# Gated delta net: one matrix for the inverses of both directions, with two products and a turn a level

## The chip, the cores and the metric

The kernel runs on one NeuronCore of one Trainium2 chip. The metric is the device time of one execution in microseconds (us). TensorE (PE in the rows) multiplies matrices and has a queue of its own for loading weights (PEld). VectorE (DVE), ScalarE (ACT) and GpSimd (POOL) do the elementwise work, and SyncE (SP) issues most DMAs. The engines run side by side and wait for one another only through semaphores.

## The reference, cut to what matters

The reference is a trunk of two layers on 512 tokens of width 1024. Layer 0 mixes tokens by windowed attention, layer 1 by a bidirectional gated delta net, and each layer ends with a mixture of 32 experts. The change lies in layer 1's token mixer. Its core is this, once forwards and once on the flipped sequence:

```python
diff = gc[..., :, None] - gc[..., None, :]
decay = jnp.where(tril, jnp.exp(jnp.where(tril, diff, 0.0)), 0.0)
kb = k * beta[..., None]
L = jnp.where(strict, jnp.einsum('bhnid,bhnjd->bhnij', kb, k) * decay, 0.0)
a_mat = L + jnp.eye(C, dtype=L.dtype)
rhs = jnp.concatenate([v * beta[..., None], kb * jnp.exp(gc)[..., None]], axis=-1)
sol = lax.linalg.triangular_solve(a_mat, rhs, left_side=True, lower=True, unit_diagonal=True)
...
def step(state, xs):
    v_new = u_i - jnp.einsum('bhck,bhkv->bhcv', w_i, state)
    o_i = jnp.einsum('bhck,bhkv->bhcv', q_i, state) + jnp.einsum('bhcs,bhsv->bhcv', a_i, v_new)
    state = state * d_i[..., None, None] + jnp.einsum('bhck,bhcv->bhkv', k_i, v_new)
```

There are 8 heads of 128 columns and two directions; the result of both scans is summed, normalised, gated by silu(z) and projected back.

## The kernel before, in words

Everything is one program in float32, with each engine's order of work written out by hand; semaphores `g[...]` join them. The delta net (functions `gdn_pe`, `gdn_act`, `gdn_pool`, `gdn_dve`) works in two halves (`hf`) of four heads. Each half has two parts.

First come 12 units (`UNITS`): q, k and v of four heads, each a projection of 24 matmuls of 512 columns, a convolution on DVE (L1478, L1481), a silu on ACT (L1343), turns on PE (L1204, L1217) and norms. The weights come in panels of 2 MB into a ring (`load_panel`, L1614); ACT and POOL or DVE split each panel into a high and a low part (L161, L167).

Then come four steps `T` of the scan (`scan_pe`, `scan_act`, `scan_pool`, `scan_dve`), with chunks of 128 tokens. A step handles the two directions `d` side by side, chunk T forwards and chunk 3-T backwards, four heads each, so that an operation on one direction has a tile of 128x512 (`[P, HH, P]`) and a bank of PSUM as its output. A step makes for each direction: the products of k with k and q with k and the decay gaps (L1233 to L1236), an exponential (L1382), masks (L1539 to L1551), two turns (L1264), and then the inverse of the unit triangular matrix by doubling blocks of 1, 2, 4 to 64 tokens, in six levels (`LEVELS` is 7). A level has three products of 128x128 for each head: L·X (L1276), a mask on DVE (L1581), then T·W (L1287) and W·T (L1289), since both the inverse (`X`) and its transpose (`T`) are kept; the last level has only the first and the third. ACT copies both results back (L1393, L1394). Last come the solve (L1297), the output (L1305) and the state's update (L1310, L1602). The next step's first products wait for the state and the output of this one.

In the second half's first step ACT and POOL also split panel `GB+7`. After the second half PE projects z in two halves of four units (L1194), while DVE, ACT and POOL normalise the output (L1496 to L1504, POOL's power L1414) and DVE gates it (L1508); then the result is turned (L257) and projected back. The layer's experts follow, whose stage the change leaves alone.

## Time and profile before

| | us |
|---|---|
| median of 3 runs (1743.88 to 1746.6) | 1746.36 |
| the profiled execution, its own time | 1746.1 |
| span of its records | 1744.5 |
| PE busy in the span | 1440.5 |
| PE busy from 787.4 to 986.5, the four steps of the first half from their first level on | 185.46 of 199.1 |

The profiled execution took 1746.1 us, 0.3 under the median, so terms read from it can be set against the median as they are. The span leaves out 1.6 us around the first and the last record. A matmul's duration in the rows is longer than the distance to the next one, since they are pipelined: the distance of starts is what one costs. The four starts that structure the text: the first half's units end at about 765.8, its four steps at 986.5 when the second half's first unit starts; the second half's units end at about 1072.1 and its steps at 1294.6.

### The profile page before, as it was taken

Reading aid. Unit: us, or ns where it says so; the run is one execution under the profiler, and the core shown is the slowest. Engines: PE = TensorE matmul, PEld = TensorE weight load, DVE = VectorE, ACT = ScalarE, POOL = GpSimd, SP = SyncE. Lnnn points to the kernel's source line nnn. Section 1 sums busy time; section 2 is a strip of 40 time slices with the busy share of each in tenths; the row PEclk is TensorE's granted clock in tenths of the full one; section 3 lists DMA queues with packets and bytes.
Section 4 is the critical chain, followed back from the end, with each engine's and each line's share of the span. In section 5 each row is a group of like instructions: output and inputs, shape, how many; then the busy total and the mean of one; then the engine's idle time right before and its main releaser. Section 6 shows DMA issues by size and latency. Waiting matters only on the chain. (4 is left out here: it accounts for less than half of the span.)

```text
span 1744.5 us, 22611 instructions
## 1 busy us (share of the span) xinstructions
PE 1440.5 (83%) x9233; PEld 1125.2 (65%) x9233; DVE 641.8 (37%) x1390; ACT 420.2 (24%) x819; POOL 394.7 (23%) x369
## 2 busy tenths in 40 slices
PE   6899995598788558889999987999999957888883
PEld 4767785355445257668888866888887754544551
DVE  3557514111111152764454376455435221111113
ACT  4246410101001123333323343333233101100110
POOL 1220003322221220521111053231114042222210
PEclk9999995699999856989999999999999958999997
DMA  5210005499999900210000012000003246999996
GB/s 183 97 49 1 19 25 217 156 386 397 397 391 399 351 31 0 92 53 1 1 1 1 1 69 77 1 1 1 1 1 109 79 162 243 390 399 394 387 411 234
DMA packets 66232, 270.87 MB, mean 155 GB/s; under 512 B 17132, under 2 KB 17388, under 8 KB 41552
## 3 DMA queue, kind: packets, MB, share of 16 engines
q1 hardware_dynamic: 49744, 237.86, 35.2%
q0 software_dynamic: 12064, 21.32, 3.6%
q10 hardware_dynamic: 4320, 10.23, 1.7%
q8 instruction: 75, 1.23, 0.3%
q14 instruction: 29, 0.24, 0.0%
HBM read 262.78 MB, written 23.35 MB: 164 GB/s over the span
## 5 line engine op out<-in xcount | busy, mean ns | idle before, releaser
L850 PE MATMUL bank<-ring,arena 128*64 128x256 f32 x2048 | 261.4, 408 | 73.1 <-issue 71.8
L850 PEld LDWEIGHTS bank<-ring,arena 128*64 128x64 f32 x2048 | 168.5, 141 | 147.0 <-issue 84.9
L735 POOL DMA_INDIRECT y_rows<-arena,idx_i x64 | 64.1, 1002 | 405.6 <-DVE arena L1008 397.6
L1289 PE MATMUL bank<-arena 128*128 128x128 f32 x768 | 140.6, 276 | 0.0
L1012 DVE TENSOR_TENSOR arena<-arena,bank 128x128 f32<-128x128 f32 x64 | 18.4, 288 | 326.3 <-ACT arena L927 326.3
L1287 PE MATMUL bank<-arena 128*128 128x128 f32 x640 | 124.5, 276 | 3.8 <-DVE arena L1581 3.8
L1581 DVE TENSOR_TENSOR arena<-bank,arena 128x512 f32<-128x512 f32 x96 | 65.5, 689 | 167.6 <-PE bank L1276 167.6
L859 PE MATMUL bank<-ring,arena 128*64 128x512 f32 x512 | 123.9, 604 | 1.5 <-DVE arena L1017 1.5
L927 ACT ACTIVATE arena<-bank 128x128 f32<-128x128 f32 x64 | 17.7, 277 | 423.5 <-PE bank L850 386.2
L1276 PE MATMUL bank<-arena 128*128 128x128 f32 x768 | 106.3, 281 | 12.7 <-ACT arena L1394 10.8
L145 PE MATMUL bank<-ring_r,ht_r 128*128 128x512 f32 x288 | 113.3, 393 | 0.0
L1289 PEld LDWEIGHTS bank<-arena 128*128 128x128 f32 x768 | 112.7, 192 | 0.7
L1276 PEld LDWEIGHTS bank<-arena 128*128 128x128 f32 x768 | 93.2, 191 | 21.8 <-ACT arena L1394 18.4
L1287 PEld LDWEIGHTS bank<-arena 128*128 128x128 f32 x640 | 97.1, 192 | 5.3 <-DVE arena L1581 5.3
L1008 DVE COPY arena<-bank 128x512 f32<-128x512 f32 x64 | 44.3, 692 | 144.7 <-PE bank L859 144.7
L167 POOL TENSOR_TENSOR ring_r<-ring,ring_r 128x1024 fp32r<-128x1024 f32 x36 | 90.5, 2538 | 25.4 <-ACT ring_r L161 25.4
L257 PE MATMUL bank<-ident,hn 128*128 128x128 f32 x192 | 40.6, 383 | 66.3 <-DVE hn L241 59.9
L143 PE MATMUL bank<-ring_r,arena_r 128*128 128x512 f32 x224 | 89.8, 401 | 4.3 <-DVE ring_r L167 4.3
L144 PE MATMUL bank<-ring_r,arena_r 128*128 128x512 f32 x224 | 88.4, 395 | 0.0
L842 PEld LDWEIGHTS bank<-ident,arena 64*128 64x128 f32 x512 | 61.3, 201 | 34.7 <-issue 25.1
L1393 ACT COPY arena<-bank 128x512 f32<-128x512 f32 x80 | 46.8, 585 | 151.6 <-PE bank L1289 151.6
L257 PEld LDWEIGHTS bank<-ident,hn 128*128 128x128 f32 x192 | 33.5, 212 | 73.1 <-DVE hn L241 56.1
(260 smaller groups left out, 2619.0 us busy)
## 6 DMA issues: line engine op xcount, KB each, us to landing
ring<-in_moe_w_gate SPq DMA_DIRECT2D x64, 1024.0 KB
ring<-in_moe_w_up SPq DMA_DIRECT2D x64, 1024.0 KB
ring<-in_moe_w_down SPq DMA_DIRECT2D x64, 1024.0 KB
ring<-in_gdn_w_in SPq DMA_DIRECT2D x8, 2048.0 KB
arena<-y_rows ACTq DMA_DIRECT2D x16, 512.0 KB, 7.4
ring<-in_attn_w_in SPq DMA_DIRECT2D x3, 2048.0 KB
ring<-in_attn_w_out SPq DMA_DIRECT2D x2, 2048.0 KB
h_rows<-hn POOLq DMA_DIRECT2D x8, 512.0 KB, 11.8
```

The costliest lines, as they stand in the source:

```text
L143: pe.matmul(dst, a[0], b[0], start=start, stop=False)
L144: pe.matmul(dst, a[0], b[1], start=False, stop=False)
L145: return pe.matmul(dst, a[1], b[0], start=False, stop=stop)
L167: eng.tensor_tensor(panel(n, False, True)[:, c, :], panel(n)[:, c, :], panel(n, True, True)[:, c, :].bitcast(F32), ALU.subtract).then_inc( ...
L257: last = pe.transpose(b[:, j * P:(j + 1) * P], hn[:, t, half * 4 + j::KC], ident[:, :])
L735: pool.indirect_dma_start(out=y_rows[l], out_offset=bass.IndirectOffsetOnAxis(ap=idx_i[:, 1, e:e + 1], axis=0), in_=y_out[:, e % RING, :], ...
L850: last = pe.matmul(bank[1][m * SLOTS:(m + 1) * SLOTS, 0:2 * P].rearrange("p (w n) -> p w n", w=2), xgt[:, i, c * SLOTS:(c + 1) * SLOTS], w ...
L859: last = pe.matmul(bank[3][half * SLOTS:(half + 1) * SLOTS, :], hidden_t[:, i, m * SLOTS:(m + 1) * SLOTS], d[:, m, half * HALF:(half + 1) ...
L1276: last = pe.matmul(bank[3 * d][:, h * P:(h + 1) * P], buf["L"][d][:, h, :], buf["X"][d][:, h, :], start=True, stop=True)
L1287: pe.matmul(bank[3 * d + 1][:, h * P:(h + 1) * P], buf["T"][d][:, h, :], buf["W"][d][:, h, :], start=True, stop=True)
L1289: last = pe.matmul(bank[3 * d + 2][:, h * P:(h + 1) * P], buf["W"][d][:, h, :], buf["T"][d][:, h, :], start=True, stop=True)
L1581: dve.tensor_tensor(buf["W"][d], heads_of(bank[3 * d]), by_head(level[l][:, d, :]), ALU.mult).then_inc(g["w"], 1)
```

## The change

One matrix per chunk and head now serves both directions: its lower triangle belongs to the forward scan and its upper to the backward one. The inverses are built apart from the scan, for two chunks at a time (two `slot`s; chunks 0 and 3, then 1 and 2), and kept with the masked q·k products in the ring's free panel. A level has one product with a masked matrix `lm` (POOL), `I - product` on DVE, a second product, and a turn of a tile `s` that ACT copies back; which half of the result goes on is chosen by two columns of constants, `stay` and `move`, one or the other for each row. `r` and `s` are updated by a copy with a factor (ACT) or a multiply by a column (POOL) and a fused multiply-add (DVE). The scan then has steps `n` without levels; step 0 has no products with the state, the last none that update it. The decays come from one product with a constant triangle for each direction and 512 columns (`rows_pe`), an exponential with beta's logarithm as its bias, and a triangular select on POOL. `w_in`'s fifth panel is loaded when the first half's scan is over, and panel `GB+7` after the second's; its split moves into the z projection. The constants and small vectors are prepared by a few other small operations, and the norm's four semaphores become two.

```diff
+        lm, w_buf, r_even, r_odd, s_buf, st_buf = [[gl.take(HH, P) for _ in range(2)] for _ in range(6)]
+        r_buf = (r_even, r_odd)
+        rhs_in, solved, q_part, e_own = w_buf, r_even, st_buf, st_buf
...
+        def kept(hf, at):
+            at = (GB + hf) % 2 * PAIR + at * HH * P
+            return flat_ring[0][:, at:at + HH * P].rearrange("p (h n) -> p h n", h=HH)
...
+                pe.wait_ge(g["kt"], 8 * (hf + 1))
+                rows_pe(pe, 4 * hf, (6, 7))
+                pe.wait_ge(g["u"], 12 * hf + 12)
+                prods_pe(pe, 4 * hf, (0, 2))
                 to_tokens_pe(pe, UNITS[12 * hf + 11])
-                for T in range(4 * hf, 4 * hf + 4):
-                    scan_pe(pe, T, hf)
-            pe.wait_ge(g["s"], 16)
+                pe.wait_ge(g["tok"], 12 * hf + 12)
+                rows_pe(pe, 4 * hf + 1, (1, 4))
+                prods_pe(pe, 4 * hf + 1, (3, 5))
+                pe.wait_ge(g["exps"], 8 * hf + 2)
+                rows_pe(pe, 4 * hf + 2, (6, 7))
+                inverse_pe(pe, 2 * hf)
+                inverse_pe(pe, 2 * hf + 1)
+                for n in range(TT):
+                    scan_pe(pe, hf, n)
...
+        def rows_pe(pe, n, banks):
+            pe.wait_ge(g["gi"], n + 1)
             for d in range(DIRS):
...
+        def prods_pe(pe, n, banks):
+            c = cols(chunk_of(n))
+            four(pe, banks[0], lambda h: k_tr[:, h, c], lambda h: k_tr[:, h, c])
+            four(pe, banks[1], lambda h: k_tr[:, h, c], lambda h: q_tr[:, h, c]).then_inc(g["prods"], 1)
...
+        def inverse_pe(pe, p):
+            first = p % 2 == 0
+            if first:
+                pe.wait_ge(g["exps"], 4 * p + 4)
+                for slot in range(2):
+                    first_m(pe, 2 * p + slot, 3 * slot + 1)
+            for l in range(1, LEVELS):
+                for slot in range(2):
+                    pe.wait_ge(g["r"], at_level(p, l, slot))
+                    pe.wait_ge(g["lm"], at_level(p, l, slot))
+                    four(pe, 3 * slot, lambda h: lm[slot][:, h, :], lambda h: r_buf[l % 2][slot][:, h, :]
+                         ).then_inc(g["y"], 1)
+                if first and l == 1:
+                    pe.wait_ge(g["exps"], 4 * p + 6)
+                    rows_pe(pe, 2 * p + 3, (6, 7))
+                if first and l == 2:
+                    pe.wait_ge(g["exps"], 4 * p + 8)
+                    prods_pe(pe, 2 * p + 2, (6, 7))
+                if first and l == 4:
+                    pe.wait_ge(g["a"], 2 * p + 3)
+                    prods_pe(pe, 2 * p + 3, (6, 7))
+                for slot in range(2):
+                    if l >= 2:
+                        pe.wait_ge(g["sn"], at_level(p, l - 1, slot))
+                        if l == 2 and not first:
+                            pe.wait_ge(g["se"], at_level(p - 1, LEVELS - 1, slot))
+                        turn_four(pe, 3 * slot + 2, s_buf[slot]).then_inc(g["t"], 1)
+                    elif not first:
+                        last_m(pe, p - 1, slot)
+                for slot in range(2):
+                    pe.wait_ge(g["wc"], at_level(p, l, slot))
+                    if l >= 2:
+                        pe.wait_ge(g["se"], at_level(p, l - 1, slot))
+                    four(pe, 3 * slot + 1, lambda h: st_buf[slot][:, h, :], lambda h: w_buf[slot][:, h, :]
+                         ).then_inc(g["un"], 1)
+            for slot in range(2):
+                if first:
...
+        def scan_pe(pe, hf, n):
+            if n == 0:
+                pe.wait_ge(g["se"], 24 * hf + 24)
+            else:
+                for d in range(DIRS):
+                    c = cols(chunk(n, d))
+                    pe.wait_ge(g["s"], 6 * hf + 2 * (n - 1) + d + 1)
+                    pe.wait_ge(g["o2"], 8 * hf + 2 * (n - 1) + d + 1)
+                    four(pe, 4 * d, lambda h: k_tr[:, h, c], lambda h: state[:, d, h * P:(h + 1) * P]
+                         ).then_inc(g["ks"], 1)
+                for d in range(DIRS):
+                    c = cols(chunk(n, d))
+                    if n >= 2:
+                        pe.wait_ge(g["qc"], 6 * hf + 2 * (n - 2) + d + 1)
+                    four(pe, 4 * d + 1, lambda h: q_tr[:, h, c], lambda h: state[:, d, h * P:(h + 1) * P]
+                         ).then_inc(g["qs"], 1)
             for d in range(DIRS):
...
+                if n:
+                    pe.wait_ge(g["rr"], 6 * hf + 2 * (n - 1) + d + 1)
+                four(pe, 4 * d + 2, lambda h: inverse_of(hf, d)[:, h, :],
+                     lambda h: rhs_in[d][:, h, :] if n else v_tok2[:, h, chunk(n, d), :]).then_inc(g["ys"], 1)
+            if n < TT - 1:
+                for d in range(DIRS):
+                    pe.wait_ge(g["kd"], 6 * hf + 2 * n + d + 1)
+                    pe.wait_ge(g["yc"], 8 * hf + 2 * n + d + 1)
+                    four(pe, 4 * d + 3, lambda h: k_decayed(hf, d)[:, h, :], lambda h: solved[d][:, h, :]
+                         ).then_inc(g["su"], 1)
             for d in range(DIRS):
...
+                pe.wait_ge(g["yc"], 8 * hf + 2 * n + d + 1)
+                four(pe, 4 * d, lambda h: a_kept(hf, chunk(n, d), d)[:, h, :], lambda h: solved[d][:, h, :]
+                     ).then_inc(g["av"], 1)
...
-                    elif t in (1, 2):
-                        split_high(act, GB + 8, (2 * t - 2, 2 * t - 1))
+                    if t in (1, 2):
+                        split_high(act, GB + 7 + half, (2 * t - 2, 2 * t - 1))
...
+        def inverse_act(act, p):
+            first = p % 2 == 0
+            for l in range(1, LEVELS):
+                if l < LEVELS - 1:
+                    for slot in range(2):
+                        act.wait_ge(g["r"], at_level(p, l, slot))
+                        if l >= 2:
+                            act.wait_ge(g["rb"], at_level(p, l - 1, slot))
+                        act.activation(flat(r_buf[(l + 1) % 2][slot]), flat(r_buf[l % 2][slot]), ACT.Copy,
+                                       scale=stay[:, l:l + 1]).then_inc(g["ra"], 1)
+                if first and l == 1:
+                    exps_act(act, 2 * p + 3, (6, 7))
+                for slot in range(2):
+                    if l >= 2:
+                        act.wait_ge(g["t"], at_level(p, l - 1, slot))
+                        act.copy(flat(st_buf[slot]), bank[3 * slot + 2][:, :]).then_inc(g["se"], 1)
+                    elif not first:
+                        last_m_act(act, p - 1, slot)
+            if not first:
+                for slot in range(2):
+                    last_m_act(act, p, slot)
...
+        def keep_pool(pool, p, l, slot):
+            pool.wait_ge(g["r"], at_level(p, l, slot))
+            if l >= 2:
+                pool.wait_ge(g["t"], at_level(p, l - 1, slot))
+            elif p % 2:
+                pool.wait_ge(g["t"], at_level(p - 1, LEVELS - 1, slot))
+            if l < LEVELS - 1:
+                pool.tensor_scalar(s_buf[slot], r_buf[l % 2][slot], move[:, l:l + 1], None, ALU.mult
+                                   ).then_inc(g["rb"], 1)
+            else:
+                pool.affine_select(out=s_buf[slot], in_=r_buf[l % 2][slot], compare_op=ALU.not_equal, fill=0.0,
...
+                        if not first:
+                            pool.wait_ge(g["y"], at_level(p - 1, LEVELS - 1, slot))
+                    else:
+                        pool.wait_ge(g["y"], at_level(p, l - 1, slot))
+                    pool.tensor_tensor(lm[slot], lt_of(n), by_head(level[l]), ALU.mult).then_inc(g["lm"], 1)
+                if l >= 2:
+                    for slot in range(2):
+                        keep_pool(pool, p, l - 1, slot)
+                if first and l == 1:
+                    spread_pool(pool, 2 * p + 3)
+                    select_pool(pool, 2 * p + 2)
+                if first and l == 3:
+                    select_pool(pool, 2 * p + 3)
+                if first and l in (4, 6):
+                    diag_pool(pool, 2 * p + l // 2)
+            for slot in range(2):
...
+        def scan_pool(pool, hf, n):
+            if n == 0:
+                pool.wait_ge(g["se"], 24 * hf + 24)
             for d in range(DIRS):
...
+                if n:
+                    pool.wait_ge(g["ys"], 8 * hf + 2 * (n - 1) + d + 1)
+                triangle(pool, inverse_of(hf, d), m_kept(hf, chunk(n, d)), d).then_inc(g["xs"], 1)
...
+                first_r(dve, n + 1, 4)
+            third, fourth = 2 * p + 2, 2 * p + 3
+            for l in range(1, LEVELS):
+                for slot in range(2):
...
+                    o.step(sum_e(dve, fourth))
+                if first and l == 5:
+                    make_a(dve, fourth, 7, 0)
+                if l < LEVELS - 1:
+                    for slot in range(2):
+                        dve.wait_ge(g["un"], at_level(p, l, slot))
+                        dve.wait_ge(g["ra"], under_six(p, l, slot))
+                        r = flat(r_buf[(l + 1) % 2][slot])
+                        dve.scalar_tensor_tensor(out=r, in0=bank[3 * slot + 1][:, :], scalar=move[:, l:l + 1], in1=r,
+                                                 op0=ALU.mult, op1=ALU.add).then_inc(g["r"], 1)
+                    for slot in range(2):
+                        dve.wait_ge(g["rb"], at_level(p, l, slot))
+                        dve.scalar_tensor_tensor(out=flat(s_buf[slot]), in0=bank[3 * slot + 1][:, :],
+                                                 scalar=stay[:, l:l + 1], in1=flat(s_buf[slot]),
+                                                 op0=ALU.mult, op1=ALU.add).then_inc(g["sn"], 1)
+                else:
+                    for slot in range(2):
+                        dve.wait_ge(g["un"], at_level(p, l, slot))
+                        dve.wait_ge(g["rb"], at_level(p, l, slot))
+                        dve.tensor_tensor(flat(s_buf[slot]), bank[3 * slot + 1][:, :], flat(s_buf[slot]), ALU.add
...
             sp.wait_ge(s["up"], 30)
...
-                load_panel(sp, GB + 6 + i, w_in[:, :, at:at + PANEL], (g["proj"], 20 + 4 * i))
+                load_panel(sp, GB + 6 + i, w_in[:, :, at:at + PANEL], ((g["proj"], 20), (g["av"], 16))[i])
...
```

## Rows read from the trace of the kernel before

**Rows 1.** The page: busy time of the engines, the slices of PE and its clock
```profile
PE 1440.5 (83%) x9233; PEld 1125.2 (65%) x9233; DVE 641.8 (37%) x1390; ACT 420.2 (24%) x819; POOL 394.7 (23%) x369
PE   6899995598788558889999987999999957888883
PEclk9999995699999856989999999999999958999997
```

**Rows 2.** Windows: stretch, its length, busy time (records) of PE, PEld, DVE, ACT, POOL, clock, DMA
```profile
765.90:787.40 21.50, 14.45 (x105) 13.43 (x105) 13.28 (x31) 4.86 (x7) 2.42 (x3) 0.84 0.28 98
787.40:986.50 199.10, 185.46 (x1570) 178.15 (x1569) 87.85 (x222) 64.11 (x117) 32.32 (x30) 1.00 0.00 1
852.40:858.30 5.90, 5.63 (x51) 5.44 (x50) 2.42 (x6) 2.15 (x4) 0.00 (x0) 1.00 0.01 4
```

**Rows 3.** Timeline of PE, one level to the next, and turns: start, us, line, records
```profile
852.46 1.06 PE L1276 MATMUL bank<-arena 128*128 128x128 f32 x8
853.79 1.16 PE L1276 MATMUL bank<-arena 128*128 128x128 f32 x8 [0.27 <-ACT arena L1394]
...
858.36 1.06 PE L1276 MATMUL bank<-arena 128*128 128x128 f32 x8
...
839.08 1.06 PE L1264 MATMUL bank<-ident,arena 128*128 128x128 f32 x8 [0.70 <-DVE arena L1551]
839.98 1.06 PE L1276 MATMUL bank<-arena 128*128 128x128 f32 x8
```

**Rows 4.** Timeline of PE in the expert stage: float32 products of 512 columns
```profile
401.04 1.94 PE L859 MATMUL bank<-ring,arena 128*64 128x512 f32 x8
402.90 0.33 PE L892 MATMUL bank<-ident,arena 128*128 128x128 f32 x1
```

**Rows 5.** Timeline of DVE and ACT in the same level
```profile
853.56 0.69 DVE L1581 TENSOR_TENSOR arena<-bank,arena 128x512 f32<-128x512 f32 x1 [2.74 <-PE bank L1276]
...
852.66 0.58 ACT L1393 COPY arena<-bank 128x512 f32<-128x512 f32 x1 [0.71 <-PE bank L1289]
853.14 0.59 ACT L1394 COPY arena<-bank 128x512 f32<-128x512 f32 x1
```

**Rows 6.** Timelines of DVE, with POOL's splits beside it and without; and both engines
```profile
1004.75 1.47 DVE L1478 TENSOR_SCALAR arena<-arena 128x512 f32<-128x512 f32 x1 [0.45 <-ACT arena L1335]
1006.25 4.34 DVE L1481 SCALAR_TENSOR_TENSOR arena<-arena 128x512 f32<-128x512 f32 x3
1022.01 0.48 DVE L1478 TENSOR_SCALAR arena<-arena 128x512 f32<-128x512 f32 x1
1022.53 2.33 DVE L1481 SCALAR_TENSOR_TENSOR arena<-arena 128x512 f32<-128x512 f32 x3
...
789.64 0.68 DVE L1581 TENSOR_TENSOR arena<-bank,arena 128x512 f32<-128x512 f32 x1
789.77 1.04 POOL L1429 TENSOR_TENSOR arena<-arena 128x512 f32<-128x512 f32 x1
```

**Rows 7.** Groups of POOL by line: count, busy us, mean ns
```profile
L1425 POOL TENSOR_TENSOR arena<-arena 128x512 f32<-128x512 f32 x16 | 24.6, 1537 | 2.3 <-ACT arena L1385 1.4
L1433 POOL TENSOR_TENSOR arena<-arena 128x512 f32<-128x512 f32 x16 | 16.3, 1039 | 254.7 <-ACT arena L1397 254.7
L1421 POOL TENSOR_SCALAR_AFFINE_SELECT arena<-arena 128x512 f32<-128x512 f32 x16 | 12.6, 788 | 102.2 <-DVE arena L1544 102.2
L586 POOL TENSOR_SCALAR arena<-arena 128x384 f32<-128x384 f32 x16 | 11.4, 715 | 54.5 <-DVE arena L531 53.9
L1414 POOL TENSOR_TENSOR arena<-arena,mhalf 128x8 f32<-128x8 f32 x4 | 10.2, 2546 | 20.8 <-DVE arena L1498 20.8
```

**Rows 8.** Groups of DVE and ACT with 128 columns: count, busy us, mean ns
```profile
L1602 DVE SCALAR_TENSOR_TENSOR arena<-arena,bank 128x128 f32<-128x128 f32 x64 | 18.0, 344 | 2.9 <-PE bank L1310 2.4
L927 ACT ACTIVATE arena<-bank 128x128 f32<-128x128 f32 x64 | 17.7, 277 | 423.5 <-PE bank L850 386.2 <-issue 37.3
```

**Rows 9.** Timeline between the last unit's projection and the first step
```profile
770.71 0.63 ACT L1343 ACTIVATE arena<-arena 128x512 f32<-128x512 f32 x1 [2.92 <-DVE arena L1481]
771.36 1.28 ACT L1382 ACT_TABLE_LOAD   x1
...
771.40 1.11 PE L1204 MATMUL bank<-ident,arena 128*128 128x128 f32 x4 [3.36 <-ACT arena L1343]
```

**Rows 10.** Timeline of DVE at the end of the z projection
```profile
1339.07 1.72 DVE L1508 TENSOR_TENSOR hn<-hn,arena 128x1024 f32<-128x1024 f32 x1 [3.96 <-ACT arena L1352]
```

**Rows 11.** The load of a w_in panel, 762 to 776: GB/s in 40 slices
```profile
GB/s 0 0 0 0 0 0 0 0 0 0 0 0 0 0 0 135 123 252 351 392 398 410 415 398 392 427 398 415 415 386 374 269 41 0 0 47 0 0 0 0
```

533 lines of the change are left out of this document (288 added, 245 removed), and 5 rows, old and new, of the table g.

## The prediction

> **What bounds the kernel now.** I read the page first. PE is busy 83% of the span, the other engines 22 to 37% [rows 1], and its slices are full from about 785 us to 985 and again from 1090 to 1290, where the clock stands at its higher level of 2.4 GHz. These are the eight steps of the delta net's scan. The windows say it exactly: from the first step's first level to the end of the first half PE is busy 185 of 199 us, DVE 88, ACT 64, POOL 32 [rows 2]. So this stage is PE's, and what counts is how many products it issues.
>
> The price of a product comes from the timeline of PE. Eight records of L1264 are eight turns and take 0.90 us to the next group [rows 3], so a record costs 0.11 us. A product of 128x128 is two records (768 of L1276 for 8 steps x 6 levels x 8 tiles): 0.22, four of them 0.89. One level lasts from 852.46 to 858.36, 5.90 us, with 24 products (5.34) in it; the rest is the wait for ACT's copies. A step is thus 5 x 24 + 16 products for its levels and 64 besides, 200 in all (44.5 us), plus 16 turns (1.8): 46.3. Four steps make 185, which is the window's busy time.
>
> With setup, a half costs 986.5 - 765.8 = 220.7 and 1294.6 - 1072.1 = 222.5, together 443.2 us. This is what the change can touch.
>
> **PE's work after.** For each half: 2 pairs x 6 levels x 16 products (42.7), 112 turns (12.4: 16 first, 80 within the levels, 16 last), 4 x 8 products for k·k and k·q (7.1), and the scan's 136 products (24 + 24 with the state, 32 solves, 24 updates, 32 outputs: 30.3). The decays are eight products of 512 columns; in the expert stage four such products fill 1.86 us from 401.04 to 402.90 [rows 4], so 0.93 for each chunk, 3.7. Sum 96.2 us against 185 plus its share of setup. If PE stayed the only bound, two halves would save 180 or more. But now each level is a chain through four engines, so I lay it out.
>
> **A level.** A bank is ready for DVE 1.10 after its first product starts (852.46 to 853.56) [rows 3, 5]. A DVE operation on 128x512 takes 0.69 and lets PE go after 0.73; back to back they come every 0.60, and for the multiply-add with a column I take 0.78 and 0.64, as the 128-column form is 0.05 slower than its plain neighbours at 0.29 (an estimate from L1602's 0.344) [rows 8]. ACT copies take 0.58, every 0.48, seen by PE after 0.65 [rows 5]. Let the second product of slot 0 start at A, slot 1's at A+0.89. Then `r` is updated from A+1.10 and A+1.99, the next first products start at A+1.88 and A+2.77, `s` is updated from A+2.63 and A+3.27, and the turns go at A+3.66 and A+4.10. ACT's copy of the first turn starts at A+4.31, PE sees it at A+4.96. DVE's `I - product` starts at A+3.91, is seen at A+4.64, so the copy ends last. The period is **5.0 us**, of which PE works 4.45 (16 products, 8 turns). It serves two chunks in both directions, where 5.90 served two of the four.
>
> POOL does two masked products and two multiplies by a column in a level. The nearest rows of the first are L1425 at 1.54 and L1433 at 1.04; for the second L586, 0.715 on 384 columns, so 0.95 on 512, and the select L1421, 0.79 [rows 7]. That makes 3.7 to 5.0 us, at or below the period; I take 1.2 and 0.8, because L1425 always runs beside DVE work on two SBUF tiles. I charge POOL nothing, its cover being the level itself; if a column multiply costs what L1425 costs, POOL needs 6.2 and sets the period.
>
> *Two pages against the trace.* DVE's multiply-adds on SBUF take 4.34 for three while POOL splits a panel and 2.33 when it does not; L1581, which reads one bank, takes 0.68 beside POOL's L1429 [rows 6]. The Trainium skill, "SBUF — State Buffer", "SBUF: two separate sides", says that a DVE instruction with two SBUF inputs and a GpSimd one exclude each other for their whole length. By that rule the level's six DVE operations, each with a bank as an input, run free, and the trace agrees. The Trainium skill, "GPSIMD Engine Reference", "4.1 Engine selection", speaks against this change: elementwise work on two inputs belongs on VectorE, being about twice as slow on GpSimd. With its 2.6 cycles for an element at 1.2 GHz a masked product would be 1.1 us plus dispatch (an estimate from that page), near the lower row, and the sum would stay.
>
> **A half, step by step.** Setup: as before, silu of the last unit ends at 771.34 and the exponential's table is loaded by 772.64 [rows 9]. Eight exponentials of 128 columns (0.28 each, about 0.18 apart [rows 8]) 1.5; POOL's select 0.8, two decay operands for chunk 2 2.3, the second select 1.5, DVE's sum and product 1.3, the unit diagonal and the seed 1.4, then 1.2 for two masks that stand ahead in DVE's queue and 1.3 for the first `st` and `r`: the first level starts at about 783.9, **18** after the units' end (21.7 before). The first pair: 6 x 5.0, plus what is queued between its products on PE: decays 0.9, two groups of k·k and k·q 1.8 each, and DVE's and POOL's extra operations at levels 1, 3, 5 and 6, 3.0: **37.5**. Changeover with first masks **1.6**, second pair **30**, last turns and copies **1.5**. Scan: step 0 has a select, a solve, ACT's copy, update and output, 6.5. A middle step has ten groups of four products, 8.9 on PE; the next step's first bank is freed by DVE's addition, at 9.3; two of them 18.6. The last has no update, 8.7. Sum **33.8**. Together 122.4; I add 1.6 for waits that I have not listed: **124**.
>
> **Around it.** The loads: the fifth w_in panel was loaded in the scan's shadow and is now issued when the first half's last output product is done. A panel takes about 6 us [rows 11]. Its first split stands in ACT's queue about 10 us after the next unit starts, ahead of the next unit's copy, so it costs nothing; if the load were slower by 4 us, each us more would be paid. Tail: panel `GB+7`'s low part (four operations of 2.5 us on POOL, as L167 has it) now stands ahead of the four powers of 2.55 [rows 7], and ends about 24 us after the scan. From there power, reduction and scaling, 5.2 for each of four tiles, end at 44, and four gates of 1.22 at 48.8. Before, the last gate ended at 1340.8, 46.2 after [rows 10]. So **+2.6**. The masks are made while DVE waits in the routing stage: 0. The small vectors trade a reciprocal for two or three short operations: 0.
>
> 1746.1 - 443.2 + 2 x 124 + 2.6 = **1553** (1553.5). The profiled run is 0.3 under the median, which I neglect. Changes under 0.2%, 3.5 us, can't be told from none here.
>
> **Rivals.**
> - *POOL sets the period.* The column multiply is not in the trace. At 1.54 each the level is 6.2, 24 levels x 1.2 = 29: 1582. For it: every engine now feeds the next. Against it: the select and L586 are cheap [rows 7].
> - *The chain is as slack as the old level*, 5.9 for 5.0, through waits that my table misses: 24 x 0.9 = 22, 1575.
> - *DVE and POOL exclude each other even with a bank as an input*: 3.7 + 3.6 = 7.3 a level, +55, 1608. Rows 6 speak against it.
> - *The clock.* PE idles more often. In the setup before, busy 14.5 of 21.5 us, the granted clock was 0.84 [rows 2]. If the whole stage ran at 1.2 GHz, PE's 96 become 192 and a half about 212: 1729.
> - *Loads come late*: 5 us at the second half's start and as much at the tail: 1563.
> - *Slower.* POOL has one slow operation, the power: 2.55 us for 8 columns [rows 7]. If its multiply by a column ran by such a loop, it would decide from 5.4 us on: then a level is 2 x 1.15 + 2 x 5.4 = 13.1, 24 x 8.1 = 194, and the gain is gone; beyond that it is slower, say 1760.
>
> **How the numbers follow.** Chances: forecast 0.60, POOL 0.14, slack chain 0.11, loads 0.05, exclusion 0.03, clock 0.04, slow multiply 0.03. Low end: levels at PE's own 4.45 (-13) and none of the unlisted waits (-3): 1537, taken as 1534. High end: POOL's 1582 with 8 for loads, 1590. That leaves out the last three cases and the edges of the others, less than 2 in 10. Faster: all but the last and a little of the clock's, 0.96; same 0.01; slower 0.03.
>
> **What would show it.** In the profile after: in the second pair of each half a level every 5.0 us with PE busy 4.45; first products after the units' end by 18 us; a middle scan step of 9.3; POOL's masked product near 1.2 and column multiply near 0.8; the stretch between units and next stage 124 instead of 221; the expert stages unchanged. I am wrong if the masked or column operations on POOL are above 1.25 on average, if `y` waits for POOL rather than for DVE, or if the clock in the stage is well under 1.

## The result and the profile after

The changed kernel takes 1589.24 us (median of 4 runs, 1584.3 to 1591.8) where the kernel before, timed beside it, takes 1746.32. The ratio is 0.910, 95% interval 0.9076 to 0.9124. It is faster by 157 us, where 193 were forecast. It stands within the range, 0.8 us under its upper end of 1590, and 36 us above the forecast. The profiled execution was the fastest of the four, 1584.3 us, span 1582.7; all that is read from it below stands against 1553, a miss of 31.

The page of the changed kernel, first its engines, its slices and its chain (compare [rows 1]):

```profile
PE 1276.8 (81%) x7601; PEld 950.4 (60%) x7601; DVE 631.7 (40%) x1196; ACT 382.8 (24%) x796; POOL 523.1 (33%) x476
...
POOL 1321001332212114024788336786350342221210
PEclk8999999589999995589899999899989669999997
...
PE bank L865 8%; PE bank L874 4%; PE bank L1286 2%; PE bank L857 2%; PE bank L143 1%; PE bank L144 1%; PE bank L145 1%; POOL arena L1566 1%; DMA arena<-y_rows 1%; DVE hn L1700 1%; POOL arena L1529 1%; PE bank L907 0%; POOL arena L719 0%; DVE hn L1696 0%; POOL slot_table L728 0%
```

PE is nearly as full as before over the whole span (81% for 83), but POOL is now at seven and eight tenths in two stretches where it was nearly idle, and POOL's L1566, the new column multiply, stands in the chain that ended last. Now the stage cut into its parts (windows: busy time of PE, weight loads, DVE, ACT, POOL, granted clock; compare [rows 2]):

```profile
765.90:788.20 22.30, 13.41 (x60) 8.83 (x61) 17.70 (x22) 10.27 (x29) 14.66 (x15) 0.86 0.01 1
788.20:832.50 44.30, 38.20 (x279) 34.89 (x277) 33.39 (x49) 13.85 (x28) 37.44 (x31) 0.91 0.00 1
832.50:867.20 34.70, 31.59 (x248) 28.08 (x248) 24.41 (x36) 14.85 (x24) 29.12 (x23) 1.00 0.00 1
867.20:902.00 34.80, 32.17 (x273) 31.03 (x273) 17.40 (x54) 10.89 (x32) 15.84 (x18) 1.00 0.00 1
844.84:850.39 5.55, 5.07 (x42) 4.52 (x41) 4.10 (x6) 2.50 (x4) 5.55 (x6) 1.00 0.00 0
850.39:855.94 5.55, 5.08 (x42) 4.53 (x41) 4.10 (x6) 2.50 (x4) 5.55 (x6) 1.00 0.00 0
883.46:893.28 9.82, 9.40 (x81) 9.08 (x81) 5.53 (x19) 3.24 (x10) 3.67 (x4) 1.00 0.01 2
```

The four first rows are the terms of my sum for one half. Forecast and measured, in us:

| term | forecast | measured |
|---|---|---|
| setup, to the first product of a level | 18 | 22.3 |
| first pair and changeover | 37.5 + 1.6 | 44.3 |
| second pair, last turns and copies | 30 + 1.5 | 34.7 |
| scan | 33.8 | 34.8 |
| waits not listed | 1.6 | - |
| first half | 124 | 136.1 |

The second half with its projections went from 308.1 us (986.5 to 1294.6) to 222.9 (902.0 to 1124.9), 85.2 saved for 98.5 forecast; the first half saved 84.6 for 96.7. What follows the delta net's last step took 449.9 before (1294.6 to 1744.5) and takes 457.8, which is +7.9 for the +2.6 forecast. So 25 us are missing in the two halves and 5 behind them.

The windows show one thing more. The granted clock stands at 0.50, that is 1.2 GHz, from 785.5 to 792.3, after a stretch in which PE was mostly idle, and the first products of a level fall into it; shorter falls follow. Windows of the changed kernel, in the same form: the first products, the sixth level of the first pair with the next one, in the first and the second half, and the stretch from the second pair's last masked product to the half's end, in the first and the second half:

```profile
788.24:791.66 3.42, 3.42 (x18) 3.42 (x17) 1.78 (x3) 0.72 (x1) 3.42 (x4) 0.50 0.00 0
817.86:833.74 15.88, 12.12 (x89) 11.24 (x87) 14.15 (x22) 3.23 (x7) 10.31 (x10) 0.89 0.00 1
1039.56:1055.00 15.44, 10.73 (x89) 9.69 (x87) 14.34 (x22) 3.23 (x7) 10.76 (x9) 1.00 0.01 2
855.93:901.97 46.04, 41.51 (x344) 38.84 (x343) 24.83 (x65) 15.02 (x39) 22.76 (x25) 1.00 0.00 1
1077.22:1124.87 47.65, 43.14 (x344) 40.46 (x343) 24.79 (x61) 16.30 (x40) 22.83 (x25) 0.96 0.00 1
```

Sixteen records take 3.42 us in the first row, where 0.11 each makes 1.78; the second half has the same. The two levels cost 0.44 more where the clock fell, and the scan 1.6. Together this is some 5 us of the 25 (an estimate from these rows: 2 x 1.64, 0.44 and 1.61).

In the table of seven windows further up, the fifth and sixth rows each show one level of the second pair: 5.55 us, and POOL busy in all of it. The timelines of that level say what it does and who waits for it:

```profile
845.73 0.66 PE L1291 MATMUL bank<-ident,arena 128*128 128x128 f32 x4 [0.48 <-DVE arena L1786]
846.32 4.05 PE L1286 MATMUL bank<-arena 128*128 128x128 f32 x32
...
844.92 0.75 DVE L1786 SCALAR_TENSOR_TENSOR arena<-bank,stay,arena 128x512 f32<-128x512 f32 x1 [0.66 <-POOL arena L1566]
845.59 1.28 DVE L1769 TENSOR_TENSOR arena<-ident,bank 128x512 f32<-128x512 f32 x2
847.52 1.64 DVE L1782 SCALAR_TENSOR_TENSOR arena<-bank,move,arena 128x512 f32<-128x512 f32 x2 [0.65 <-PE bank L1286]
...
844.84 2.52 POOL L1591 TENSOR_TENSOR arena<-ring,arena 128x512 f32<-128x512 f32 x2
847.32 3.12 POOL L1566 TENSOR_SCALAR arena<-arena,move 128x512 f32<-128x512 f32 x2
```

POOL goes from two masked products (2.52 us) straight to two column multiplies (3.12) and from there to the next level, with no gap. DVE's update of `s` waits 0.66 us for the multiply, and PE's turn waits 0.48 for that update. The multiply costs twice what I gave it (`count | busy us, mean ns`):

```profile
L1566 POOL TENSOR_SCALAR arena<-arena,move 128x512 f32<-128x512 f32 x40 | 63.2, 1595 | 2.6 <-PE bank L1291 2.6
L1591 POOL TENSOR_TENSOR arena<-ring,arena 128x512 f32<-128x512 f32 x48 | 62.0, 1317 | 8.1 <-PE bank L1286 8.1
```

### The profile page after: what moved, and what is told of

The parts are those of the page before. It is cut to its first block and busy times, and to the rows that moved or that the text cites. A ratio compares the mean times of both kernels' runs of the same rounds, so it can differ in the third digit from the quotient of the medians.

```text
span 1582.7 us, 19352 instructions
## 1 busy us (share of the span) xinstructions
PE 1276.8 (81%) x7601; PEld 950.4 (60%) x7601; DVE 631.7 (40%) x1196; ACT 382.8 (24%) x796; POOL 523.1 (33%) x476
## 5 line engine op out<-in xcount | busy, mean ns | idle before, releaser
L1286 PE MATMUL bank<-arena 128*128 128x128 f32 x1088 | 140.4, 286 | 14.3 <-DVE arena L1769 6.5
L1286 PEld LDWEIGHTS bank<-arena 128*128 128x128 f32 x1088 | 131.7, 198 | 26.6 <-DVE arena L1769 10.0
L167 POOL TENSOR_TENSOR ring_r<-ring,ring_r 128x1024 fp32r<-128x1024 f32 x36 | 93.9, 2632 | 34.8 <-ACT ring_r L161 34.8
L1023 DVE COPY arena<-bank 128x512 f32<-128x512 f32 x64 | 44.3, 692 | 144.6 <-PE bank L874 144.6
L257 PEld LDWEIGHTS bank<-ident,hn 128*128 128x128 f32 x192 | 33.8, 213 | 84.1 <-DVE hn L241 58.5
L857 PEld LDWEIGHTS bank<-ident,arena 64*128 64x128 f32 x512 | 61.3, 201 | 34.7 <-issue 25.1
L1673 DVE SCALAR_TENSOR_TENSOR arena<-arena 128x512 f32<-128x512 f32 x72 | 80.9, 1123 | 2.6
L144 PE MATMUL bank<-ht_r,ring_r 128*128 128x512 f32 x192 | 78.0, 406 | 0.0
L857 PE MATMUL bank<-ident,arena 64*128 64x64 f32 x512 | 70.1, 278 | 9.3 <-DMA arena<-h_rows,idx_i 9.3
L743 POOL DMA_INDIRECT arena<-h_rows,idx_i x64 | 60.7, 948 | 25.7 <-issue 18.9
L229 POOL TENSOR_TENSOR norm_s<-norm_s,mhalf 128x1 f32<-128x1 f32 x16 | 8.9, 556 | 171.3 <-DVE norm_s L238 171.3
L1591 POOL TENSOR_TENSOR arena<-ring,arena 128x512 f32<-128x512 f32 x48 | 62.0, 1317 | 8.1 <-PE bank L1286 8.1
```

The costliest lines, as they stand in the source:

```text
L144: pe.matmul(dst, a[0], b[1], start=False, stop=False)
L167: eng.tensor_tensor(panel(n, False, True)[:, c, :], panel(n)[:, c, :], panel(n, True, True)[:, c, :].bitcast(F32), ALU.subtract).then_inc( ...
L257: last = pe.transpose(b[:, j * P:(j + 1) * P], hn[:, t, half * 4 + j::KC], ident[:, :])
L857: last = pe.transpose(bank[0][:, c * SLOTS:(c + 1) * SLOTS], xg[0:SLOTS, i, c::KC], ident[0:SLOTS, 0:SLOTS])
L1286: last = pe.matmul(bank[b][:, h * P:(h + 1) * P], lhs(h), rhs(h), start=True, stop=True)
L1591: pool.tensor_tensor(lm[slot], lt_of(n), by_head(level[l]), ALU.mult).then_inc(g["lm"], 1)
```

## The experiments

The rival "POOL sets the period" looked true at this point, and its price, 29 us, looked like the whole miss. The first experiment tests it; the others take the remaining places where the windows show lost time. Each is timed beside the kernel before, and since the runs come from different chips, I compare ratios: two of them can be told apart from about 0.0021 on, 3.7 us.

**The changed kernel again**, as the yardstick.

> The changed kernel once more, as the yardstick for the runs beside it: 1584 to 1592 us, ratio to the kernel before 0.910.

1587.44 us, ratio 0.9081 (0.9067 to 0.9096). From the first masked product of the first pair to that of the second pair: 44.4 us, and 44.6 in the second half; the second pair's levels 5.56.

**The column multiply on ACT.**

```diff
-                pool.tensor_scalar(s_buf[slot], r_buf[l % 2][slot], move[:, l:l + 1], None, ALU.mult
+            act.activation(flat(s_buf[slot]), flat(r_buf[l % 2][slot]), ACT.Copy, scale=move[:, l:l + 1]
```

> The column multiply that keeps part of the matrix at a level (POOL, two a level, 1.6 us each) is done by ACT with a column as its scale; POOL keeps the masked product alone (two of 1.26). If POOL's 5.6 us a level set the 5.55 us period, the levels of the second pairs come every 5.0 to 5.1 us (PE's own records fill 5.07 of the 5.55), those of the first pairs lose 1 us and more each, and the kernel gains 12 to 20 us: 1567 to 1575. If the chain of matmul, DVE and turn sets it and POOL is only busy beside it, the period stays within 0.1 us of 5.55 and the time within 2 us of the changed kernel's. If ACT becomes the bound (4.1 us of work a level by the rows after), the period stays above 5.3.

1584.20 us, 0.9065 (0.9049 to 0.9081): 2.8 us by the ratios, which alone could be nothing. The trace is clear, though. Timelines of POOL and of PE's and ACT's part in one level:

```profile
846.93 2.52 POOL L1602 TENSOR_TENSOR arena<-ring,arena 128x512 f32<-128x512 f32 x2 [2.71 <-PE bank L1286]
852.16 2.51 POOL L1602 TENSOR_TENSOR arena<-ring,arena 128x512 f32<-128x512 f32 x2 [2.71 <-PE bank L1286]
...
848.95 4.03 PE L1286 MATMUL bank<-arena 128*128 128x128 f32 x32 [0.33 <-ACT arena L1488]
...
849.17 1.34 ACT L1568 ACTIVATE arena<-arena,move 128x512 f32<-128x512 f32 x2
```

The level now comes every 5.23 us and POOL waits 2.71 in it. So POOL did set the period, but the next bound stands only 0.32 us behind it. In the first pair nearly nothing changed: 44.0 and 43.6 us for 44.4 and 44.6. My expectation of 12 to 20 us was wrong there. The rival's mechanism is real and its price is not: something else holds the first pair. One part of that is the clock. The second level of the first pair, in the two halves of this same run:

```profile
794.26:800.80 6.54, 6.54 (x37) 4.93 (x36) 2.41 (x5) 2.94 (x10) 2.49 (x3) 0.81 0.00 0
1015.86:1020.87 5.01, 5.01 (x34) 3.92 (x34) 2.42 (x5) 2.94 (x10) 2.50 (x3) 1.00 0.00 0
```

PE is busy in all of both, and the one at the lower clock takes 1.5 us more.

**What makes the multiply dear.** First a constant for the column (the kernel then leaves out the choice of rows, and only its times mean anything), then, with the column back, a second step that adds zero, then both.

```diff
-                pool.tensor_scalar(s_buf[slot], r_buf[l % 2][slot], move[:, l:l + 1], None, ALU.mult
+                pool.tensor_scalar(s_buf[slot], r_buf[l % 2][slot], 0.5, None, ALU.mult
```

> POOL's column multiply takes the constant 0.5 instead of the column of the level, so the inverse is wrong and only times are read. If reading the multiplier from a column is what costs, the operation falls from 1.56 us (3.12 for two) to near my 0.8, POOL has 4.1 us a level and the level comes every 5.2 us as it did with the multiply on ACT: 3 us gained. If 128x512 costs 1.56 in any form, nothing changes: 1587.

```diff
-                pool.tensor_scalar(s_buf[slot], r_buf[l % 2][slot], move[:, l:l + 1], None, ALU.mult
+                pool.tensor_scalar(s_buf[slot], r_buf[l % 2][slot], move[:, l:l + 1], 0.0, ALU.mult, ALU.add
```

> The same column multiply on POOL, written as multiply by the column and then add 0.0, the form of the 384-column operation that I priced it by (0.51 us at its fastest; only that form's second step differs). The result is the same. If the form with a second step is the cheap one on POOL, the operation falls from 1.58 us to 0.7 to 0.8, POOL has 4.1 us a level, and the level comes every 5.2 us: 3 us gained, as with the multiply on ACT. If a second step adds work, it is 1.6 us or more and the level 5.6 or longer: 1587 or more.

> Multiply by the constant 0.5 and add 0.0 (the inverse is wrong, only times are read): exactly the form of the 384-column operation. If the row's price carries over by columns, 0.7 to 0.8 us. If it stays at 1.5, that row was cheap for another reason than its form.

The line's own view (minimum, median and maximum in ns, then who waited for it), first of the constant without a second step, then of the column with one, then of the constant with one:

```profile
L1566 POOL TENSOR_SCALAR arena<-arena x40: 1481/1491/1928, 796.3 to 1084.0; 128x512 f32<-128x512 f32 x40
```

```profile
L1566 POOL TENSOR_SCALAR arena<-arena,move x40: 688/697/1135, 794.3 to 1078.8; 128x512 f32<-128x512 f32 x40
```

```profile
L1566 POOL TENSOR_SCALAR arena<-arena x40: 612/621/1057, 796.4 to 1082.3; 128x512 f32<-128x512 f32 x40
```

Reading the multiplier from a column costs 0.08 us (0.70 to 0.62, or 1.58 to 1.49). The missing second step costs 0.87: `multiply` is slower than `multiply, then add 0.0`. The row by which I priced the operation, L586 in [rows 7], has a second step, and the diff's line has `None` there. The times: 0.9066 (0.905 to 0.9083) for the constant with levels of 5.39 us; 1581.13 us, 0.9043 (0.9017 to 0.9069) for the column with the second step, levels of 5.23 as on ACT, and nobody waits for POOL's multiply any more; the last one had one run, 1585.18, levels 5.23. One argument in one line gives 6.6 us with an interval of about 5. In the traces it does what the multiply on ACT did: from the last projection's end to the next stage the halves take 134.5 and 135.1 us here, 134.4 and 135.0 there. So 6.6 and 2.8 are two readings of one gain.

The Trainium skill, "GPSIMD Engine Reference", "4.1 Engine selection", says that against VectorE GpSimd is about twice as slow with two tensor inputs and roughly at line rate with one. By that rule the multiply would be well below the masked product. These runs agree when the operation has its second step (0.62 to 0.70 for 1.28) and contradict it when it has not (1.49 to 1.58, above the masked product).

**DVE's extra work in the first pair.** PE's timeline of the yardstick in the last levels of the first pair, and DVE's:

```profile
812.24 2.05 PE L1286 MATMUL bank<-arena 128*128 128x128 f32 x16 [1.27 <-DVE ring L1730]
...
822.47 4.06 PE L1286 MATMUL bank<-arena 128*128 128x128 f32 x32 [2.02 <-DVE arena L1769]
...
828.93 0.38 PE L1286 MATMUL bank<-arena 128*128 128x128 f32 x1 [1.53 <-DVE arena L1769]
...
819.54 0.68 DVE L1727 TENSOR_TENSOR ring<-bank,ring 128x512 f32<-128x512 f32 x1
820.14 1.68 DVE L1735 TENSOR_TENSOR ring<-ring,arena 128x512 f32<-128x512 f32 x1
821.74 1.27 DVE L1769 TENSOR_TENSOR arena<-ident,bank 128x512 f32<-128x512 f32 x2
```

The product of the fourth chunk's k·k with its decay (L1727) and the third chunk's seed (L1735) stand in DVE's queue ahead of `I - product` (L1769), for which PE waits 2.02 us. The seed has two SBUF inputs and takes 1.68 for 0.68, as POOL's masked products run from 818.77 to 821.27. Seven of the ten extra operations stand like this between the update of `s` and the next `I - product`. The edit moves them behind L1769, where DVE waits for PE anyway, and the fourth chunk's two decay products into the second pair. It also moves PE's two groups for the fourth chunk behind the second products of the fourth level; the two moves were not tried apart. Cut to a part:

```diff
-                if first and l == 4:
-                    make_lt(dve, fourth, 6)
-                    make_v0(dve, third)
...
+                if first and l == 5:
+                    make_lt(dve, fourth, 6)
+                    make_v0(dve, third)
...
+                if not first and l == 2:
+                    make_a(dve, 2 * p + 1, 7, 0)
```

> The ten DVE operations on the third and fourth chunk that stand within the first pair's levels move to where DVE waits for the second product of a level (two of them into the second pair's levels), and PE's products for the fourth chunk move behind the level's last ones. From the first masked product to the second pair's first masked product the changed kernel takes 44.4 us. If DVE's queue order is what makes these levels long (waits of 1.3, 2.0 and 1.5 us of PE for it), it takes 40 us or less, and the kernel gains 7 to 10 us: near 1579. If POOL or PE's own extra products set them, it stays above 43 and the time within 3 us of 1587.

1578.53 us, 0.9035 (0.9022 to 0.9047): 8.0 us faster than the yardstick, the largest single gain. The pair takes 41.9 and 41.4 us for 44.4 and 44.6, so 2.6 and 3.2 gained, with the clock at 0.92 in all four: less than expected within the pair. The rest is not in these levels. From the second pair's last masked product to the end of the first half, the yardstick and then this run:

```profile
856.47:903.99 47.52, 42.98 (x344) 40.34 (x343) 24.82 (x65) 15.02 (x39) 22.85 (x25) 0.96 0.00 1
854.93:900.96 46.03, 41.50 (x344) 38.83 (x343) 24.83 (x65) 15.02 (x39) 22.79 (x25) 1.00 0.00 1
```

The work is the same and the clock is not, and the second half shows the same 1.5 us. The changed kernel's own trace has this stretch once at 46.0 and once at 47.7, so it is not the edit's doing as far as the traces show. DVE's order, with PE's, is worth some 6 of the 8 us.

**POOL's spreads later, and another order at a half's start.**

```diff
+            if n % 4 < 2:
+                pool.wait_ge(g["conv"], 12 * hf + 11 + n % 4)
             for d in range(DIRS):
                 last = pool.tensor_tensor(e_of(n)[d], by_head(incl_of(1 - d)), col("g", c, hf, d), ALU.mult)
```

> POOL's two spreads of the gate over the triangle wait for the convolutions of the last two units. If they shut DVE out of a convolution (5.66 us for three multiply-adds, 2.33 without), the eleventh unit's convolution ends over 2 us sooner and the first levels start 1 to 1.5 us sooner in each half: 2 to 3 us gained. If the stretch is set by ACT's table load and exponentials in turn, nothing changes within 1 us, and if the second spread comes late for the second chunk's rows, up to 2 us are lost.

```diff
                 make_v0(dve, n)
-                make_a(dve, n + 1, 5, 0)
-                make_a(dve, n + 1, 5, 1).then_inc(g["a"], 1)
-                first_st(dve, n)
-                first_r(dve, n, 1)
                 make_v0(dve, n + 1)
-                first_st(dve, n + 1)
+                first_r(dve, n, 1)
                 first_r(dve, n + 1, 4)
+                first_st(dve, n)
+                first_st(dve, n + 1)
+                make_a(dve, n + 1, 5, 0)
+                make_a(dve, n + 1, 5, 1).then_inc(g["a"], 1)
```

> At the start of a half DVE makes both seeds (v0), then both first r, both first st, and only then the second chunk's two decay products. If the setup's 22.4 us were set by DVE's queue order, PE's second turn starts 2 us sooner and so do the levels: 2 to 2.5 us less from the last projection to the first product of a level in each half, 4 to 5 us in all, 1583. If ACT's exponentials and POOL's diagonal set it, less than 1 us a half.

The spreads: 1587.81 us, 0.9086 (0.9072 to 0.9099), no gain. DVE's timeline in the yardstick and in the experiment, with POOL's in the second:

```profile
762.68 5.66 DVE L1673 SCALAR_TENSOR_TENSOR arena<-arena 128x512 f32<-128x512 f32 x3
769.51 1.01 DVE L1670 TENSOR_SCALAR arena<-arena 128x512 f32<-128x512 f32 x1 [0.57 <-ACT arena L1413]
```

```profile
764.43 4.34 DVE L1675 SCALAR_TENSOR_TENSOR arena<-arena 128x512 f32<-128x512 f32 x3
769.95 1.29 DVE L1672 TENSOR_SCALAR arena<-arena 128x512 f32<-128x512 f32 x1 [0.57 <-ACT arena L1413]
...
768.92 2.04 POOL L1548 TENSOR_TENSOR arena<-arena 128x512 f32<-128x512 f32 x2 [2.27 <-DVE arena L1675]
```

The eleventh unit's multiply-adds became 1.3 us shorter (not 3.3, since a panel's low part still ran beside them), and then the twelfth unit's multiply met the spread (1.29 for 1.01) that POOL now makes from 768.92 on. The first masked product comes 18.7 and 18.5 us after the last projection's end, for 19.2 and 18.1.

The order: 0.9072 (0.9056 to 0.9087), 1.6 us by the ratios, not resolved. The first product of a level starts 2.5 us after the first masked product instead of 4.4, as expected, but the second pair then starts only 1.2 us sooner in each half. POOL's masked products of the second level start 7.0 us after those of the first in both kernels, behind a spread and two selects, so the first level gains nothing. Of the 1.2 us, 0.9 come in the second level, where the granted clock is 1.00 for 0.82. The order and the clock may hang together: in all eight halves with this order (here and in the three kernels that combine edits, below) the fall at the first products lasts 3.4 us, in 15 of the 18 halves without it 6.8. So DVE's queue did delay the first product, but what the sooner start gave by itself and what by a shorter fall of the clock was not separated.

**The tail.** Timelines of DVE and POOL in the changed kernel (compare [rows 10]):

```profile
1170.12 10.97 DVE L1700 TENSOR_TENSOR hn<-hn,arena 128x1024 f32<-128x1024 f32 x4
...
1138.59 4.77 POOL L167 TENSOR_TENSOR ring_r<-ring,ring_r 128x1024 fp32r<-128x1024 f32 x2 [15.68 <-ACT ring_r L161]
...
1148.75 1.66 POOL L1529 TENSOR_TENSOR arena<-arena,mhalf 128x8 f32<-128x8 f32 x1
...
1164.11 2.54 POOL L1529 TENSOR_TENSOR arena<-arena,mhalf 128x8 f32<-128x8 f32 x1 [2.87 <-DVE arena L1690]
1166.62 12.26 POOL L167 TENSOR_TENSOR ring_r<-ring,ring_r 128x1024 fp32r<-128x1024 f32 x4
```

POOL's powers begin 24 us after the z projection's start (1124.9), as forecast. But then the next panel's low part begins at 1166.62 and runs beside the gates: four gates take 10.97 us.

```diff
+            pool.wait_ge(g["ready"], TT)
             split_low(pool, GB + 8)
```

> POOL's low part of the first output panel (four of 2.5 to 3.1 us) waits until DVE has made the four gates. If POOL shuts DVE out of the gates (10.97 us for four, 1.1 us each without it), the gates end some 7 us sooner after the z projection's start (at +49 instead of +56), the last quarters of the panel then come about 1.5 us late for PE, and the kernel gains 4 to 6 us. If the gates are slow for another reason, they still take 11 us, and the kernel loses about 10 us, since the panel's low part comes after them.

1581.99 us, 0.9053 (0.9038 to 0.9067): 4.9 us gained. The same two engines:

```profile
1170.84 4.63 DVE L1701 TENSOR_TENSOR hn<-hn,arena 128x1024 f32<-128x1024 f32 x4
...
1175.55 9.41 POOL L167 TENSOR_TENSOR ring_r<-ring,ring_r 128x1024 fp32r<-128x1024 f32 x4 [6.07 <-DVE hn L1701]
```

Both engines are faster apart than together: 4.63 for 10.97 and 9.41 for 12.26. Each of the first three gates takes 3.25 to 3.38 beside POOL, about its own 1.16 and one subtraction's 2.35. PE's first product of the projection comes 51.6 us after the z projection's start (1127.7 to 1179.3) instead of 60.9 (1124.9 to 1185.7), and some of that is given back since the panel's low part is now late for it. The Trainium skill, "SBUF — State Buffer", "SBUF: two separate sides", says that a DVE instruction with two SBUF inputs and a GpSimd instruction that reads SBUF exclude each other for their whole length. The gates have two SBUF inputs, and this pair of runs agrees with it. So DVE and POOL wait for one another not only through semaphores. PE's waits at the turns before the projection fell too, from 9.9 us to 3.1, and with them the time at 1.2 GHz there, from 17.1 us (1171.2 to 1188.3) to 3.4.

**The four together**, with the multiply on ACT.

> The multiply on ACT, the panel's low part behind the gates, DVE's work in its waits and the start's order, together. If the four act on different stretches their gains add: 3.2 and 5.5 measured, 8 and 4.5 expected, 1566 to 1569. If the multiply on ACT was held back by DVE's extras in the first pair, up to 5 us more: 1561. If ACT becomes the bound, 1572 or more.

1565.56 us, 0.8957 (0.8939 to 0.8975), 21.7 us below the yardstick by the ratios, just under the 1566 to 1569 expected for gains that add. The single gains (2.8, 4.9, 8.0, 1.6) add up to 17, with an uncertainty of about 11, as the yardstick's own error stands in each of them; so the surplus of 4 us is not resolved. The first pair takes 37.9 us, 6.5 less than the yardstick, where the three edits that touch it gave 0.4, 2.5 and 1.2 alone. Some 1.6 of the 2.4 us that the single gains leave open sit in the second level: 6.5 us in the yardstick with the clock at 0.82, 5.6 with the start's order at full clock but with POOL's dear multiply, 5.0 with the multiply on ACT at full clock, 4.0 here. There the multiply and the late start with its slower clock had covered for each other. The other 0.8 sit in the fifth and sixth levels, where the multiply on ACT alone lost 0.7, DVE's order alone gave 2.7 and both together 2.8.

**The same with the multiply on POOL and its second step**, and then with the spreads too as multiplies by a column:

```diff
-                last = pool.tensor_tensor(e_of(n)[d], by_head(incl_of(1 - d)), col("g", c, hf, d), ALU.mult)
+                for h in range(HH):
+                    last = pool.tensor_scalar(e_of(n)[d][:, h, :], incl_of(1 - d), one("g", c, hf, d, h), 0.0,
+                                              ALU.mult, ALU.add)
```

> The four changes of the run before together, but with the multiply left on POOL and given its second step (0.70 us) instead of moved to ACT. If the level is now the chain of PE, ACT's copy and DVE, and POOL only has to be under it, the level comes every 5.23 us as with ACT, and the time is that of the run before within 2 us: 1564 to 1568.

> The same, and the spread of the gate over the triangle is made of four multiplies by a column of 128x128 with a second step instead of one product of two tiles of 128x512 (1.24 us each, 16 in all). If such a multiply is as cheap as the others here (0.7 us for 512 columns, so 0.2 to 0.3 for 128), a spread takes 0.8 to 1.1 us, and if it leaves DVE free, DVE's sum of the decays beside it takes 0.69 instead of 1.52 and the eleventh unit's last three multiply-adds 2.33 instead of 5.66: the first level starts 1 to 2 us sooner in each half, 2 to 4 us gained. If issue costs are high, four take as long as one and nothing is gained.

1565.45 us, 0.8969 (0.8957 to 0.8981), levels 5.23 and first pair 37.9: as with ACT, and as expected. With the spreads 1563.75 us, 0.8955 (0.8942 to 0.8967), 2.4 us less, within the uncertainty. The traces show no gain: the first masked product comes 0.3 to 1.0 us sooner and the first pair takes 38.7 for 37.9. Both are faster than the kernel before and the changed one. In the last of them POOL's groups, and then the timelines of POOL and DVE in the setup:

```profile
L1569 POOL TENSOR_SCALAR arena<-arena,move 128x512 f32<-128x512 f32 x40 | 29.1, 740 | 1.4 <-PE bank L1291 1.4
L1548 POOL TENSOR_SCALAR ring<-arena 128x128 f32<-128x128 f32 x48 | 21.6, 472 | 0.0
```

```profile
776.24 0.90 POOL L1548 TENSOR_SCALAR ring<-arena 128x128 f32<-128x128 f32 x1
...
776.29 0.69 DVE L1726 TENSOR_TENSOR ring<-arena 128x512 f32<-128x512 f32 x1
```

A 128-column multiply takes 0.37 us alone (the mean, 0.47, has some that waited), and four of them 1.7 to 1.9 (2.4 beside the eleventh unit's multiply-adds), more than the 1.24 to 1.46 of the product that they replace. DVE's sum beside them takes 0.69 where it took 1.52 beside the product. But DVE is not free of POOL: the multiply that started at 776.24 took 0.90, so here POOL waited for DVE's sum, and then went on. Shorter instructions changed who waits, and for how long. The expected 0.2 to 0.3 was wrong.

## Why the prediction was right and where it was wrong

**Right.** The stage was PE's, and its products were what it paid for: with the inverses of both directions in one matrix a half goes from 221 us to 136. The scan came at 34.8 for 33.8, a middle step at 9.82 for 9.3, with PE busy 9.40 of it. POOL's masked product takes 1.28 in the median, 1.32 in the mean, for 1.2. The clock stood at 0.86, 0.91 and 1.00 in the stage's parts, so the rival with the whole stage at 1.2 GHz is out; a smaller price of the clock is not (the sixth step below). Late loads are out: the second half's projections took 84.2 us for 85.9 before. DVE's six level operations, each with a bank as an input, were not held up by POOL: 1.28, 1.64 and 1.4 to 1.5 us for pairs beside a POOL that never rests, and 1.27, 1.64 and 1.40 with the multiply on ACT and POOL idle for 2.71 of 5.23.

**Luck.** The range held by 0.8 us, and not for its reasons. Its upper end was POOL's 29 and 8 for late loads; curing POOL gave 6.6 and the loads cost nothing, and terms that the range had no name for filled the place. Two of the prediction's own signs of being wrong came true: both POOL operations are above 1.25 us on average, 1.32 and 1.59.

**The step that failed first** is "for the second L586, 0.715 on 384 columns, so 0.95 on 512 ... I take 1.2 and 0.8" and with it "I charge POOL nothing". The multiply took 1.59. I scaled a row whose form was not the form of the diff. POOL then needs 5.6 us a level and set the period. The rival that says so was right in its mechanism, and its price (1.2 us for each of 24 levels, 29 us) was wrong: with the multiply at 0.70, or on ACT, the second pair's level is 5.23, so POOL cost 0.32 there, and the whole cure gave 6.6 us by one reading and 2.8 by the other.

**The second** is the period of **5.0**. It is 5.23 when POOL is out of the way. My table had every hand-over, and PE's wait for ACT's copy of the turn, 0.33, is the one that it shows too; PE's own groups follow each other with small gaps where the table had none. At 0.23 for each of 24 levels this is 5.5 us.

**The third**, and the largest that one edit gave back, is "DVE's and POOL's extra operations at levels 1, 3, 5 and 6, 3.0", in a first pair of 37.5. It took 44.3 with the changeover, for 39.1 (37.5 and 1.6). I summed durations and did not place them in the queue: seven of the operations stand between the update of one level and the first operation of the next, and PE waits for what is behind them. Their order gave 2.6 and 3.2 us back. With DVE's order, the start's and POOL's multiply mended, the stretch from masked product to masked product is 37.9 for 44.4. A second term of this pair was wrong as well, "decays 0.9": the price came from [rows 4], whose products have 64 columns of weights where these have 128. PE's rows of one chunk's decays at full clock, the next product starting at 777.36:

```profile
775.54 1.12 PE L1300 MATMUL bank<-ring,arena 128*128 128x512 f32 x2 [0.78 <-DVE arena L1707]
776.51 1.02 PE L1300 MATMUL bank<-ring,upper 128*128 128x512 f32 x2
```

That is 1.82 us for 0.93. One chunk of four is queued in the first pair, among products that PE runs without a gap from 787.34 to 799.29, and costs 0.9 more there.

**The fourth** is setup, 18 for 22.3. Eight exponentials took 2.18 us, not 1.5; the decays of three chunks took some 1.8 us of PE each, where 0.9 was my price; DVE's sum took 1.52 for 0.69 beside POOL's spread; the first turn of the second chunk waited for its seed behind two products. Later spreads and another order gave no gain that can be told from none. How the 4.3 us of a half split among these causes was not separated and stays open.

**The fifth** is the tail, +2.6 for +7.9. I had POOL's powers at the right time and then forgot what follows them on POOL: a panel's low part. Before the change it ran from 1329.2 to 1339.7 and met the last gates only for part of their time (1.49 and 1.72 us for one); now it runs beside all four without a pause. I had cited the rule that excludes the two and applied it to the levels alone. With the low part behind the gates, what follows the scan takes 449.5 us, as before the change (449.9), so the +2.6 was not needed either.

**The sixth** is the clock. The sum takes every level and the scan at 2.4 GHz, and the rival asks only about the whole stage. In the profiled execution the clock was at 1.2 GHz for some 15 us after the first product of a level in the two halves together, which can cost PE at most half of that; the rows of the section on the result show some 5. No edit tested it by itself.

## What to carry to other kernels

Price an operation by a row of exactly its form, second step included, and when there is none, keep the dear end of the range as a live case. When an engine that idled gets work, list for each of its instructions what runs beside it and who stands behind it in its queue: three of the six misses were in part order and company, not work. A measured bound is worth only its distance to the next one: removing POOL from the level gave 0.32 us of the 0.6 by which its 5.6 stood above my 5.0. And before a trace is compared with another, compare their clocks stretch by stretch: 1.5 us of a scan came and went with it in runs of one kernel.

## What the runs showed of the hardware

- On POOL a multiply of 128x512 f32 by a scalar takes 1.49 us (constant) or 1.58 (column) without a second step, and 0.62 or 0.70 with `add 0.0` behind it.
- The same multiply on 128x128 takes 0.37 us where 128x512 takes 0.70: a quarter of the columns, half of the time.
- DVE's sum of two SBUF tiles takes 0.69 us beside POOL's multiply of 128x128, and that multiply then takes 0.90 for 0.37; beside POOL's product of two 128x512 tiles the same sum takes 1.52. POOL's spread itself takes 1.02 with DVE elsewhere (2.04 for two) and 1.24 to 1.46 beside it.
- A product of 128x512 in float32 with 128 columns of weights takes 0.85 to 0.97 us at the full granted clock (two records), and 1.82 for two.
- After a stretch in which PE is mostly idle (782 to 787) the granted clock fell to 0.50 from 785.5 to 792.3, and 16 records took 3.42 us for 1.78.
